# The first block's token in PSUM for 104 of its dot products

## The reference

```python
x = layer_norm(DEEPNORM_ALPHA * x + mix, ln1_g[l], ln1_b[l])
ffn = peer(x, peer_w_query[l], peer_sub_keys[l], peer_u[l], peer_v[l])
x = layer_norm(DEEPNORM_ALPHA * x + ffn, ln2_g[l], ln2_b[l])
```

```python
u = jnp.take(expert_u, ic, axis=0)
h = jax.nn.gelu(jnp.einsum('cd,ced->ce', xc, u).astype(jnp.float32), approximate=False)
vv = jnp.take(expert_v, ic, axis=0)
return jnp.einsum('ce,ced->cd', (gc * h).astype(vv.dtype), vv)
```

## Time and profile before

| | |
|---|---|
| median of the runs | 1628.85 us (1624.02 to 1632.88) |
| profiled execution: span | 1614.6 us |
| PE busy | 1300.6 us, 81% of the span |
| DVE busy | 1140.6 us, 71% |
| POOL busy | 735.1 us, 46% |
| ACT busy | 270.3 us, 17% |
| moved by DMA | 603.45 MB, mean 374 GB/s |

### The profile page before, as it was taken

One profiled execution on the slowest core, in us unless ns is written; L12 is line 12 of the kernel. 1 busy time (PEld: TensorE's weight loads), 2 busy tenths in 40 slices (PEclk: granted clock), 3 DMA queues, 4 the chain that ended last, 5 costly groups with the idle time before them and its releaser, 6 DMA issues.

```text
span 1614.6 us, 11652 instructions
## 1 busy us (share of the span) xinstructions
PE 1300.6 (81%) x3512; PEld 625.1 (39%) x3512; DVE 1140.6 (71%) x2715; ACT 270.3 (17%) x766; POOL 735.1 (46%) x645
## 2 busy tenths in 40 slices
PE   8979979986879896787878787777777879787886
PEld 5466436533334554333333332333333323333332
DVE  1349999877888869977676768676767686764544
ACT  0100000122222111121212121212121212121111
POOL 0005456677656455553544343544444445343430
PEclk9989999998989998897989888999998898898899
DMA  9948789899889978999999999999999999999992
GB/s 340 390 149 319 306 287 357 349 407 354 283 286 342 353 279 336 421 422 422 422 421 422 421 421 422 421 422 421 422 421 421 421 422 422 422 422 422 421 422 118
DMA packets 125710, 603.45 MB, mean 374 GB/s; under 512 B 12624, under 2 KB 14928, under 8 KB 76368
## 3 DMA queue, kind: packets, MB, share of 16 engines
q0 software_dynamic: 92160, 536.91, 82.4%
q1 hardware_dynamic: 33488, 65.80, 11.1%
HBM read 600.57 MB, written 2.10 MB: 373 GB/s over the span
## 4 chain that ended last, share of the span: by engine, by line
DMA 40%; DVE 24%; PE 22%; POOL 7%; issue 4%; SPq 1%; ACT 1%; DVEq 0%; POOLq 0%
DMA arena<-uv,idx 38%; PE W L512 7%; POOL arena L475 5%; DVE arena L1095 5%; PE ACC L512 4%; PE W L547 2%; PE W L553 2%; PE W L791 2%; DVE xs L1087 2%; DVE arena L1073 2%; DVE cand L1341 1%; DVE cand L1343 1%; DVE sel L1345 1%; PE ACC L499 1%; DMA arena<-peer_w_query 1%
## 5 line engine op out<-in xcount | busy, mean ns | idle before, releaser
L1095 DVE SCALAR_TENSOR_TENSOR arena<-arena,xs 128x1024 f32<-128x1024 f32 x384 | 466.6, 1226 | 294.2 <-DMA arena<-uv,idx 292.4
L461 POOL DMA_INDIRECT arena<-uv,idx x384 | 432.7, 1127 | 527.4 <-PE W L512 305.9
L512 PE MATMUL W<-arena,fdiag 128*128 128x512 f32 x1024 | 504.2, 653 | 143.8 <-ACT fdiag L1025 143.7
L475 POOL DMA_INDIRECT arena<-uv,idx x232 | 272.9, 1176 | 287.6 <-DVE idx L1351 125.8
L512 PEld LDWEIGHTS W<-arena,fdiag 128*128 128x128 f32 x1024 | 210.3, 209 | 437.0 <-issue 256.1
L512 PE MATMUL ACC<-arena,fdiag 128*128 128x512 f32 x512 | 250.5, 651 | 73.6 <-ACT fdiag L1025 73.6
L512 PEld LDWEIGHTS ACC<-arena,fdiag 128*128 128x128 f32 x512 | 105.3, 209 | 218.9 <-issue 129.0
L1025 ACT ACTIVATE fdiag<-ident,gate 128x128 f32<-128x128 f32 x384 | 123.2, 390 | 356.8 <-DVE gate L1102 356.0
L1073 DVE SCALAR_TENSOR_TENSOR arena<-arena,xs 128x1024 f32<-128x1024 f32 x128 | 151.6, 1225 | 22.9 <-DMA arena<-uv,idx 22.2
L547 PE MATMUL W<-arena 128*128 128x512 f32 x320 | 142.5, 601 | 8.5 <-DMA arena<-w_in 7.8
L1087 DVE SCALAR_TENSOR_TENSOR xs<-arena,gate,xs 128x1024 f32<-128x1024 f32 x80 | 102.7, 1284 | 29.6 <-DMA arena<-uv,idx 23.3
(11 more groups left out here) (184 smaller groups left out, 884.1 us busy)
## 6 DMA issues: line engine op xcount, KB each, us to landing
arena<-w_in SPq DMA_DIRECT2D x13, 2048.0 KB, 12.9
arena<-peer_w_query SPq DMA_DIRECT2D x8, 2048.0 KB, 17.0
arena<-uv,idx POOLq DMA_INDIRECT x616, 25.7
arena<-w_out SPq DMA_DIRECT2D x4, 2048.0 KB, 15.8
arena<-w_in SPq DMA_DIRECT2D x4, 512.0 KB, 6.6
out<-xs SPq DMA_DIRECT2D x4, 512.0 KB, 7.9
arena<-xT SPq DMA_DIRECT2D x1, 1536.0 KB, 19.9
xs<-x SPq DMA_DIRECT2D x1, 1536.0 KB, 17.1
```

What stands on the lines that cost most here:

```text
L461: pool.indirect_dma_start(out=fused[slot], out_offset=None, in_=uv, in_offset=bass.IndirectOffsetOnAxis(ap=idx[:, E + n:E + n + 1], axis=0 ...
L475: pool.indirect_dma_start(out=ring[r], out_offset=None, in_=rows, in_offset=bass.IndirectOffsetOnAxis(ap=idx[:, e:e + 1], axis=0), element ...
L512: last = nc.tensor.matmul(sum_of(b)[:, half * HW:(half + 1) * HW], fdiag[:, n % ND, :], fused[n % NS][:, D + half * HW:D + (half + 1) * HW ...
L1095: STT(out=fused[slot][:, 0:D], in0=fused[slot][:, 0:D], scalar=1.0, in1=xs[:, b, :], op0=ALU.mult, op1=ALU.mult, accum_out=hid[:, E + n:E ...
```

## The change

A copy of block 0's token is made once on ACT, from `xs[:, 0, :]` into the two banks of X, after `take_x1(0)` and before `query(0)`; it signals `token_ready`. The first dot waits for that in place of `x1_ready`. Dots 0 to 103 read the token in X, dots 104 to 127 in `xs` as before. `out_part(1, 0)`, the first matmul that writes X after the copy, now waits until dot 103 was done.

```diff
+        TOKEN_DOTS = 104
...
                     if b > 1:
                         pe.wait_ge(x1_taken, 2 * b)
+                    elif half == 0:
+                        r, count = slot_of("U", TOKEN_DOTS - 1)
+                        pe.wait_ge(slot_used[r], count)
...
             take_x1(0, out_banks(0))
+            nc.scalar.activation(X[:], xs[:, 0, :], ACT.Copy).then_inc(token_ready, 1)
             query(0, WAVES[0])
...
                 if e == 0:
-                    dve.wait_ge(x1_ready, 1)
+                    dve.wait_ge(token_ready, 1)
                 p = AT["U", e // HALF]
                 r = ring_slots(p)[e % HALF]
                 dve.wait_ge(row_landed[r], landed(p))
-                STT(out=ring[r], in0=ring[r], scalar=1.0, in1=xs[:, 0, :], op0=ALU.mult, op1=ALU.mult,
+                STT(out=ring[r], in0=ring[r], scalar=1.0, in1=X[:] if e < TOKEN_DOTS else xs[:, 0, :], op0=ALU.mult, op1=ALU.mult,
                     accum_out=hid[:, e:e + 1]).then_inc(slot_used[r], 1)
```

More of the change, by code:

```diff
@@ L319, in build @@
         gelu_ready = sem("gelu_ready")
+        token_ready = sem("token_ready")
         gate_exp_ready = sem("gate_exp_ready")
```

## The result

The change made the kernel slower, by about 5 us. Its median is 1633.24 us (1623.08 to 1638.38, 20 runs) beside 1627.55 us for the kernel before (1621.27 to 1639.85, 20 runs); the ratio is 1.0032, 95% interval [1.0018, 1.0047]. Forecast were 8 us less. The execution that was profiled has a span of 1634.9 us and a device time of 1636.73 us.

What follows compares the result with a forecast made beforehand. POOL's gather issue, held by SBUF-reading dots, was taken to bound 320 to 392 us; gains of 2.6 and 6.2 us, capped by DMA at 8.3, less 0.3 for misfits, gave 8 us: 1628.85 to 1620.9 us, range 1614 to 1629.5.

Steps and rivals of the forecast that it cites:

- second gain: 320 to 392 us: POOL's gathers, no longer held by dots, save 6.2 us that pass through; bounds 0 and 7.6.
- DVE's saved waits reappear later as waits for PE: A sign named beforehand, for the whole kernel, that would show the forecast of 8 us less to be wrong.
- 329.6 less 328.9: Eighth gather after 320.22 us: PE frees its slot at 329.6, unhindered start 328.9; 0.8 us put as lost.
- What bounds the stretch: 320 to 392 us: POOL's issue sets the time; 38 gathers to 375.0 take 7.6 us too much, held by dots.
- Copy, and the wait of out_part(1, 0): ACT's copy fits in idle time, PE's wait before block 2's attention is always over: 0 us each.
- The dot: Dots 0 to 103: the same time from PSUM as from SBUF, 1221 ns median; upper bound +0.12 us each.
- First gain: Before 248 us: faster gathers remove DVE's dot waits of 2.4 us and 0.2 of smaller gaps, 2.6 us in all.
- 248 to 317 us: DVE ends this part 5.3 us ahead of PE, so what gathers save here is worth nothing by itself.
- What DMA allows: 288.4 to 396.44 us: DMA traffic lets the dot at 396.44 come at most 8.3 us sooner.
- The sum's base: Whole kernel: span 1614.6 us, with the runs' median 14.25 us above it and the same distance taken after.
- weights late: Rival: tighter gather bursts delay w_in slices for PE by 5.0 us each, 25 over five; time 1646 us, chance 0.05.
- 0.08 for slower: Chance that the whole kernel measures slower: late weight slices and some of the cases of a dearer dot.

Runs made afterwards that it cites:

- the second trace of before: The kernel before, unchanged, run and traced once more: 1626.52 us, ratio 0.9986 to its other runs, span 1619.5 us.
- the two breaks: Changed kernel, POOL waiting ahead of the 57th gather for three retention scores and the 129th for block 1's turned mixed output: 1621.06 us, ratio 0.9956 to the kernel before.
- short ones: Changed kernel with eight small memsets on POOL, each waited for, ahead of every fourth gather from the 49th to the 152nd: 1626.96 us, ratio 0.9998 to the kernel before.
- the breaks and dots in SBUF: Kernel with the two breaks, but all dots reading the token in SBUF, the copy kept: 1635.30 us, ratio 1.0029 to the kernel before.

## Why the prediction was wrong

The step that failed is the second gain, 6.2 us, that was to pass through to the end; the stretch before it, put at nothing, failed as well. One of the signs of being wrong that the prediction named came true: "DVE's saved waits reappear later as waits for PE". The sums can be followed as written but for one: 329.6 less 328.9 is 0.7, not 0.8.

*What bounds the stretch.* Right as a reading of before: POOL's issue, held by dots with both inputs in SBUF; the gathers under dots in PSUM took 0.94 us. Too strong was that gathers of 1.99 are the rule under a dot: from 320 to 375 us 23 gathers began under one, 4 took over 1.9 us, and the mean was 1.24. The total of 7.6 us was read rightly.

*Copy, and the wait of out_part(1, 0): 0.* Not contradicted: 0.9994 [0.9974, 1.0014] for both together.

*The dot: no difference.* Right: 1217 ns. By the estimate from the figures of the Trainium skill (VectorE: DVE Perf Modes, The TRN2 errata) 65 ns more had been due; the trace does not agree, and the measurement decides.

*First gain, 2.6 us.* Right in mechanism: none of the dot waits of 2.4 us in the earlier trace rows is left up to 248 us, and with 48 dots PE's fill of 248.16 began at 248.76, where the second trace of before has it at 252.43. Its size is not shown: 0.9984 x 1628 is 2.6 less, in an interval that reaches over 1.

*248 to 317 us, "worth nothing by itself".* Wrong, and it is the first place of the loss. I took that faster gathers could only be idle gain there. They were a loss: 48th to 60th gather went out one each 1.24 us, the signal of a retention score came 8.6 us late and cost DVE 4.1, and the 65th and 73rd gather, which need slots that DVE frees after them, fell 6 and 9 us back (the expectations above count from 0 and call them 64 and 72). POOL waited 27.8 us for dots from 250 to 306 us (after), and 12.3 from 240 to 292 before:

```profile
POOL arena L478 <- DVE arena L1080: 27.8, 6, 12.1
```

*Second gain, 6.2 us, of which I wrote that "the saving passes through".* This is the step that failed. Its first half held: 38 gathers took 35.95 us, where 38 x 0.94 = 35.7 had been put. Its second half did not: the step that DVE makes between dot 103 and the next dot waits for a score of PE, and that score hung on a signal from PE to ACT that was 13 us late. I had asked what DVE waits for and priced it by the rows; I had not asked what else passes between the engines while POOL has no gap. With the two breaks the kernel gains 6.7 us where the sum had 8; that these are the terms of the sum is not shown, as no trace shows where they lie.

*What DMA allows, 8.3 us.* Not put to the test by the change: the share was 1.02 from 332 to 383 us, as forecast, but the score was later than any row. The gain of the kernel with two breaks, 6.7, does not pass it.

*The rivals.* None named it. The one on the slower side, weights late, did not happen: from 137 to 330 us PE has no wait for w_in in the trace after. (Landings can't be read there, as records are missing; before, the slices issued from 130 to 340 us landed in 7.7 to 18.7 us, against a limit of 23.5.) The chance of 0.08 for slower was too small for a change that takes away the pauses of an engine whose rows most of the others work on. The first trace of before had no late signal in it, so the price could not have been read there; that a side effect unpriced may exist could.

*The sum's base.* 14.25 us between span and device time was the luck of a quick execution. It did not enter the difference.

**What is shown and what is not.** Shown: with the breaks absent, the loss comes with dots 48 to 103 in PSUM, or with either half of them. It comes with signals of PE and DVE that are late by up to 16.5 us, by the records of the increments. Two stops of POOL, or short ones, remove both the late turn and the loss.

Not shown: what keeps the signals. A full DMA is not enough: from 295 to 375 us the first trace before has a DMA share of 1.03 and no late signal. The pace of POOL alone is not enough either, as the seven gathers at 124 and at 128 us show, and no length of a row of gathers parts the cases: with dots 48 to 75 the turn came 15.2 us late after rows of 10 and 9 gathers at 1.24 us, with the breaks and dots in SBUF the product came 10.8 us late after rows of 10 and 6.

The largest rival left is the recording itself. Every run here was recorded: each has its span and granted clock. In the first trace before all increments are on record (14504 records, of which 11088 = 16 x 693 are those of DMAs), none is late, and the execution was quicker than all others of its kernel. In each of the 14 other traces, the second one of the same kernel too, 1365 to 1893 of them are missing, and in each the hand-over from PE to ACT before the first dot was late by 2.8 to 4.1 us, where the first trace has 0.0. They go missing in the stretches with late signals: of the 15 rows that POOL issued from 375.89 to 395.80 in the changed kernel, 68 of 240 increments are on record. Against it as the whole cause: most are missing with the two breaks (1893), the fastest kernel. The Trainium skill (NOTIFIC — Programmer's Manual, When the ring fills) says that a queue of records that is full can drop new ones or hold up its producer; the missing records fit the first, and no run here shows whether the second happened. So it is open whether the changed kernel is slower at all when nothing is recorded.

Open too is why the 104 dots cost less (5 us) than dots 48 to 75 alone (11 us), more than the 2.6 us of the first gain explain.

## What to carry to other kernels

When a change takes away the pauses of an engine that issues many small gathers, ask what passes between the other engines in those pauses, and not only what the engine itself gains. A step in a trace that begins 5 us or more after the recorded end of what it waits for may hang on a late signal: look for the increment's own record, then stop the issuer once, just before that hand-over, and see if the wait goes. Look at how long that stop became, too: placed behind a late signal it costs what the signal is late. And take two traces of the kernel before; one may be of a quick execution, or the only one with all its records.

## What the runs showed of the hardware

- 104 multiply-and-accumulate instructions of 128x1024 took 1217 ns with one input in PSUM and 1218 to 1221 with both in SBUF, and let gathers of 0.94 us pass; those under SBUF dots took up to 1.99.
- While POOL issued gathers one every 1.24 us, in rows of 7 to 21, signals of PE and DVE were on record and reached their waiters up to 16.5 us after the recorded ends; with 0.09 us more for each gather still 13.7 for the second half of the turn; with 1.27 us more every fourth, 0.1 for the turn. All of this is in traces with missing records; in the one trace without, no increment was more than 0.03 us late.
- In the changed kernel the late signals of the turn came after a pause of POOL: on record at 398.99 and 399.05, where POOL's last gather before had ended at 396.74.
- Increments by DMAs in the same stretch were not late, as far as they are on record: for the rows issued from 376 to 396 us the last recorded one came 4.0 to 6.7 us after the issue, beside landings of 6.5 to 7.0 us in the first trace before (rows issued at 353 and 363 us).
